# Weaving an expert pair's scatter between the w1/w3 products of the next pair

## What is computed

```python
def _routed_experts(h, expert_id, gate, w1, w3, w2):    # 32 experts, D_EXPERT = 512, 2 experts a token
    ...
    def expert_block(args):
        tok, e, g = args
        xb = h[tok]
        y = (jax.nn.silu(xb @ w1[e]) * (xb @ w3[e])) @ w2[e]
        return (y * g[:, None]).astype(h.dtype)
    ...
    return jnp.zeros_like(h).at[buf_tok].add(y.reshape(P, D))
```

## Time and profile before

| | |
|---|---|
| median of three timed runs | 3413.08 us |
| profiled execution, span | 3411.1 us |
| TensorE busy (products) | 3186.5 us, 93% |
| VectorE, ScalarE, GpSimd busy | 1083.0, 945.4, 884.8 us |
| chain that ended last | TensorE 79%, issue 8%, VectorE 7%, GpSimd 4% |
| expert loop, first w1/w3 load to the last add | about 2735 to 3310 us |

### The profile page before, as it was taken

How to read it: one execution, slowest core, us unless ns; L and a number is a source line. 1 busy time by engine, 2 the same in 40 slices (tenths; PEclk the granted TensorE clock), 3 DMA queues, 4 the chain that set the end, 5 groups by cost and what they waited for, 6 DMA issues and landing times.

```text
span 3411.1 us, 44591 instructions
## 1 busy us (share of the span) xinstructions
PE 3186.5 (93%) x18030; PEld 2437.0 (71%) x18030; DVE 1083.0 (32%) x1746; ACT 945.4 (28%) x1583; POOL 884.8 (26%) x499
## 2 busy tenths in 40 slices
PE   6799999999899999999999999999796899999998
PEld 4687887888788888777888777888573655545543
DVE  2406645112311111141654123212268222222324
ACT  3124444212321122233444233222323111111121
POOL 3331000333322322443100444444564200000000
PEclk9899999999999999998999999999798799999998
DMA  6322221111111111212311222232220478888840
GB/s 208 109 83 92 93 87 57 62 68 62 50 62 51 67 67 52 71 51 82 97 63 56 93 86 86 83 109 83 71 92 13 179 304 363 363 332 363 342 197 25
DMA packets 65557, 415.61 MB, mean 122 GB/s; under 512 B 7648, under 2 KB 9072, under 8 KB 21520
## 3 DMA queue, kind: packets, MB, share of 16 engines
q1 hardware_dynamic: 57600, 393.77, 30.3%
q0 software_dynamic: 5232, 15.64, 2.0%
q10 hardware_dynamic: 2592, 4.34, 0.3%
HBM read 411.61 MB, written 9.96 MB: 124 GB/s over the span
## 4 chain that ended last, share of the span: by engine, by line
PE 79%; issue 8%; DVE 7%; POOL 4%; ACT 2%; ACTq 0%; DMA 0%; POOLq 0%; DVEq 0%
PE ps L500 42%; PE ps L848 7%; PE ps L633 5%; PE ps L648 4%; PE ps L823 4%; PE ps L871 3%; PE ps L671 3%; POOL half_slots L1337 3%; DVE second_block L1798 2%; PE ps L655 2%; PE ps L916 2%; PE ps L888 2%; PE ps L528 2%; DVE X L1971 1%; PE ps L517 1%
## 5 line engine op out<-in xcount | busy, mean ns | idle before, releaser
L500 PE MATMUL ps<-h_parts,half_slots 128*128 128x512 f32 (+1 forms) x6240 | 1230.4, 359 | 68.9 <-POOL half_slots L1337 37.8
L500 PEld LDWEIGHTS ps<-h_parts,half_slots 128*128 128x128 f32 x6240 | 1037.8, 190 | 263.6 <-issue 62.0
L1337 POOL TENSOR_TENSOR half_slots<-ring,half_slots 128x1024 fp32r<-128x1024 f32 (+3 forms) x292 | 630.5, 2160 | 1352.2 <-ACT half_slots L983 1351.9
L983 ACT ACTIVATE half_slots<-ring 128x1024 fp32r<-128x1024 f32 (+3 forms) x292 | 280.3, 961 | 1362.6 <-PE ps L500 1351.7
L500 PE MATMUL ps<-hidden_parts,half_slots 128*128 128x512 f32 (+1 forms) x1584 | 305.1, 355 | 0.0
L500 PEld LDWEIGHTS ps<-hidden_parts,half_slots 128*128 128x128 f32 x1584 | 261.0, 188 | 43.6
L500 PE MATMUL ps<-y_parts,half_slots 128*128 128x512 f32 (+1 forms) x1152 | 230.4, 361 | 10.2 <-DVE y_parts L1652 9.7
L500 PEld LDWEIGHTS ps<-y_parts,half_slots 128*128 128x128 f32 x1152 | 193.9, 192 | 44.7 <-issue 12.0
L848 PE MATMUL ps<-second_block,scratch 128*64 128x512 f32 x1024 | 223.3, 593 | 1.1 <-DVE scratch L1942 0.6
L633 PE MATMUL ps<-half_slots,q_parts 64*128 64x512 f32 (+1 forms) x576 | 183.3, 366 | 6.4 <-DVE na_k_lower L1598 6.2
L1325 POOL COPY second_block<-second_block 128x512 f32<-128x512 f32 x4 | 2.5, 628 | 700.4 <-ACT second_block L952 700.4
(11 more groups left out here) (262 smaller groups left out, 3257.3 us busy)
## 6 DMA issues: line engine op xcount, KB each, us to landing
second_block<-experts SPq DMA_DIRECT2D x192, 1024.0 KB, 7.9
ring<-stream SPq DMA_DIRECT2D x146, 1024.0 KB, 4.8
ring<-stream SPq DMA_DIRECT2D x16, 768.0 KB, 4.1
ring<-stream SPq DMA_DIRECT2D x16, 640.0 KB, 3.8
ring<-stream SPq DMA_DIRECT2D x16, 512.0 KB, 3.4
bias_rows<-rpb POOLq DMA_DIRECT2D x2, 3840.0 KB, 32.6
first_block<-bias_rows POOLq DMA_DIRECT2D x32, 224.0 KB, 4.2
second_block<-w_gate SPq DMA_DIRECT2D x4, 1024.0 KB, 8.0
```

What stands on the lines that cost most here:

```text
L500: last = nc.tensor.matmul(ps[s % 2][:, a:b], part(x, s)[:, k, :], parts[y][:, tile + k, a:b], start=start and k == 0 and n == 0, stop=stop ...
L983: act.activation(part(0, s), raw_half(s), ACT.Copy).then_inc(hi_done, 1)
L1337: nc.gpsimd.tensor_tensor(part(1, s), raw_half(s), part(0, s).bitcast(fp32), ALU.subtract)\
```

## The change

The scatter of pair p is taken out of turn p and put into turn p + 1, on TensorE and on VectorE. On TensorE two tiles of it follow each of the four groups of w1/w3 products: tiles 0 and 1 behind the first, 6 and 7 behind the last. Turn 0 stands ahead of the loop, with nothing to weave; the loop runs `rest` = total - 1 turns; the scatter of the last pair stands behind it, and waits for both copies of the gathered tokens before tile 0. On VectorE a turn begins with the eight adds of the pair before, then come the picks (now of the same turn), GH, the lower part, the copy of gathered tokens, and the selection. `rest` is written into a second element of `total_i` by one more small operation, and TensorE and VectorE read it. ScalarE, GpSimd and SP keep their code.

```diff
--- before.py
+++ after.py
@@ -167,7 +167,7 @@
         es.enter_context(nc.sbuf_tensor("common_memory", [P, 42496], fp32))
         gate = sb("gate", [P, 4, NE])
         pos = sb("pos", [P, 4, NE])
-        total_i = nc.sbuf_tensor("total_i", [P, 1], mybir.dt.int32)
+        total_i = nc.sbuf_tensor("total_i", [P, 2], mybir.dt.int32)
         total_i = es.enter_context(total_i)
         lam8 = sb("lam8", [P, 8, 4])
         vec = sb("vec", [P, NV])
@@ -815,7 +815,8 @@
             pe.wait_ge(htk_a, 4)
             pe.wait_ge(htk_v, 4)
             pe.wait_ge(r_ok, 1)
-            total = pe.value_load(total_i[0:1, 0:1], min_val=PAIRS, max_val=PAIRS * (NL // CAP))
+            rest = pe.value_load(total_i[0:1, 1:2], min_val=PAIRS - 1, max_val=PAIRS * (NL // CAP) - 1)
+            total = rest + 1
 
             def gather(half):
                 for k in range(4 * half, 4 * half + 4):
@@ -833,7 +834,21 @@
             gather(0)
             gather(1)
             turn_selection()
-            with pe.Fori(0, total) as i:
+
+            def scatter(p, tiles):
+
+                for m in tiles:
+                    if m == 0:
+                        pe.wait_ge(m_pick, p + 1)
+                        pe.wait_ge(m_ysv, p + 1)
+                    if m >= 2:
+                        pe.wait_ge(m_add, 8 * p + m)
+                    for x in range(2):
+                        last = nc.tensor.matmul(ps[0][:, 512 * (m % 2):512 * (m % 2) + 512],
+                                                YP[x][:, m // 4, (m % 4) * P:(m % 4 + 1) * P], PICK, start=x == 0, stop=x == 1)
+                    last.then_inc(m_sc, 1)
+
+            def expert_pair(i, before=None):
                 pe.wait_ge(m_xga, i + 1)
                 pe.wait_ge(m_xgv, i + 1)
 
@@ -849,6 +864,8 @@
                                                         XG[:, 4 * kk + k, x * CAP:(x + 1) * CAP], w,
                                                         start=kk == 0 and k == 0, stop=kk == 1 and k == 3)
                         last.then_inc(m_steps, 2)
+                        if before is not None:
+                            scatter(before, (2 * (2 * w13 + kk), 2 * (2 * w13 + kk) + 1))
 
                 pe.wait_ge(m_sel, i + 2)
                 pe.wait_ge(m_add, 8 * i + 1)
@@ -875,19 +892,14 @@
                 gather(1)
 
                 pe.wait_ge(m_w, i + 1)
-                pe.wait_ge(m_pick, i + 1)
                 turn_selection()
 
-                pe.wait_ge(m_ysv, i + 1)
-                for m in range(KD):
-                    if m < 2:
-                        pe.wait_ge((m_xga, m_xgv)[m], i + 2)
-                    if m >= 2:
-                        pe.wait_ge(m_add, 8 * i + m)
-                    for x in range(2):
-                        last = nc.tensor.matmul(ps[0][:, 512 * (m % 2):512 * (m % 2) + 512],
-                                                YP[x][:, m // 4, (m % 4) * P:(m % 4 + 1) * P], PICK, start=x == 0, stop=x == 1)
-                    last.then_inc(m_sc, 1)
+            expert_pair(0)
+            with pe.Fori(0, rest) as i:
+                expert_pair(i + 1, i)
+            pe.wait_ge(m_xga, rest + 2)
+            pe.wait_ge(m_xgv, rest + 2)
+            scatter(rest, range(KD))
 
 
             pe.wait_ge(p_in, 32)
@@ -1915,11 +1927,13 @@
             link(nc.vector.tensor_tensor(passes, passes, gmax[:, 0:1].to_broadcast([P, 8]), ALU.is_lt))
             link(nc.vector.tensor_reduce(gmax[:, 1:2], passes, AX.X, ALU.add))
             link(nc.vector.tensor_scalar(gmax[:, 2:3], gmax[:, 1:2], float(PAIRS), None, ALU.mult))
-            nc.vector.tensor_copy(total_i[:, :], gmax[:, 2:3]).then_inc(r_ok, 1)
+            link(nc.vector.tensor_scalar(gmax[:, 3:4], gmax[:, 2:3], -1.0, None, ALU.add))
+            nc.vector.tensor_copy(total_i[:, :], gmax[:, 2:4]).then_inc(r_ok, 1)
 
 
             dve.wait_ge(r_ok, 1)
-            total = dve.value_load(total_i[0:1, 0:1], min_val=PAIRS, max_val=PAIRS * (NL // CAP))
+            rest = dve.value_load(total_i[0:1, 1:2], min_val=PAIRS - 1, max_val=PAIRS * (NL // CAP) - 1)
+            total = rest + 1
             iota = cst[:, CST["iota"]:CST["iota"] + CAP]
             sel4 = SEL.rearrange("p (c x n) -> p c x n", c=4, x=2)
             selg4 = SELG.rearrange("p (c x n) -> p c x n", c=4, x=2)
@@ -1953,10 +1967,16 @@
                 nc.vector.tensor_tensor(selg4, sel4, wts[:, :, :, None].to_broadcast(shape4), ALU.mult).then_inc(m_sel, 1)
                 nc.vector.tensor_scalar(two, two, -float(CAP), None, ALU.add).then_inc(m_dec, 1)
 
-            gathered(1)
-            picks(1)
-            select_next(1)
-            with dve.Fori(0, total) as i:
+            def add_to_x(p):
+                for m in range(KD):
+                    dve.wait_ge(m_sc, 8 * p + (m + 1))
+                    nc.vector.tensor_tensor(X[:, m, 0:NL], ps[0][:, 512 * (m % 2):512 * (m % 2) + 512], X[:, m, 0:NL],
+                                            ALU.add).then_inc(m_add, 1)
+
+            def expert_pair(i, before=None):
+                if before is not None:
+                    add_to_x(before)
+                picks(i + 1)
                 dve.wait_ge(m_act, i + 1)
                 dve.wait_ge(m_steps, 12 * i + 8)
                 nc.vector.tensor_tensor(GH, ps[1][:, 512:1024], SGM, ALU.mult).then_inc(m_g, 1)
@@ -1966,13 +1986,14 @@
                                                scalar=wslot[:, 0:1], in1=YP[0].bitcast(fp32), op0=ALU.mult,
                                                op1=ALU.subtract).then_inc(m_ysv, 1)
                 gathered(i + 2)
-                for m in range(KD):
-                    dve.wait_ge(m_sc, 8 * i + (m + 1))
-                    nc.vector.tensor_tensor(X[:, m, 0:NL], ps[0][:, 512 * (m % 2):512 * (m % 2) + 512], X[:, m, 0:NL],
-                                            ALU.add).then_inc(m_add, 1)
-                picks(i + 2)
                 select_next(i + 2)
 
+            gathered(1)
+            select_next(1)
+            expert_pair(0)
+            with dve.Fori(0, rest) as i:
+                expert_pair(i + 1, i)
+            add_to_x(rest)
 
             dve.wait_ge(m_add, 8 * total + 1)
             plain_norm(7, "g_ple")
```

## The result

The changed kernel took 3428.65 us (median of 5 runs, 3427.98 to 3430.26), the kernel before beside it 3413.88 (3411.9 to 3415.94): a ratio of 1.0043, 95% interval 1.003 to 1.0055. That is 14.8 us slower; forecast were 3427 and 13.9.

The account below looks back on a forecast made before the run. TensorE, in its order, was taken to set the 35.84 us turn. Terms of 21.03 against 20.24 us gave +0.79 a turn, +11.9 over 15 turns, +2.0 once: +13.9 on the 3413.08 median, 3427 us; range 3414 to 3440.

Parts of the forecast that it names:

- the top: Start of a turn: first w1/w3 product waits for VectorE's gathered-token copy, 1.05 us after the turning's first load.
- four groups of w1/w3: The w1/w3 run cut in four groups of 3.60 us: 14.41 us a turn, the cutting costing 0.50.
- three middle scatters: Four scatter products behind each of the first three w1/w3 groups, 1.15 us each with array-shape switches: 3.45 a turn.
- tiles 6 and 7 and the wait for their adds: Fourth scatter, from tile 6's load to gather(0)'s: 2.12 us for 0.93 us of products.
- the loop entry: Entering the loop of turns: 0.27 us counted once, rounded to +0.3 in the once-per-run sum.
- Rival 1: Array-shape switches between scatter and w1/w3 cost nothing: -0.39 us a turn, 3409 us, no measurable change; chance 0.12 with neighbours.
- The wait at gather(0): gather(0) needs tile 6's bank and waits for all eight adds; some 1.2 us a turn stay on the path.
- Rival 3: The wait at gather(0) costs 0.6 us, not 1.2: 0.19 a turn stays, 3418 us; chance 0.09.
- Rival 2: TensorE's instruction stream falls behind at computed waits: 1.35 us more a turn, 3447 us; chance 0.12, in part or whole.
- Work beside other work: Picks, gated hidden values, selection, silu and weight transfers lie beside other work, at no cost.
- Once per run: Last scatter's first add later by 1.5 us, new small operation +0.2, loop entry +0.3: +2.0 once.
- ring: Scatter tiles wait for adds to free two PSUM banks: 2.2 us of the 5.89 us scatter, which a weave would hide.

Follow-up runs that it names:

- e1: The changed kernel with the waits for the two weight slots put ahead of the waits for the gathered-token copies at a turn's top: 3424.69 us, ratio 1.0029.
- e5: The changed kernel with the weave one group earlier: tiles 0 and 1 ahead of the first w1/w3 group, 6 and 7 behind the third: 3403.37 us, ratio 0.9969.
- e3: The kernel before plus one useless full-width product behind each of the first three groups of w1/w3: 3442.78 us, ratio 1.0084.
- e4: The kernel before plus one useless half-width product behind each of the first three groups of w1/w3: 3424.99 us, ratio 1.0034.
- e7: The changed kernel with a finer weave, one scatter tile behind each of eight half groups of w1/w3: 3448.87 us, ratio 1.0096.
- e2: The changed kernel with scatter tiles in the two ps[2] banks, the wait for adds moved from gather(0) to before w2: 3412.44 us, ratio 0.9994.
- e6: The kernel before, without weave, its scatter using four PSUM banks in place of two: 3385.53 us, ratio 0.9915.

## Why the prediction was right, point by point

| from the turning's first load to gather(0)'s | forecast | measured |
|---|---|---|
| the top, to the first w1/w3 load | 1.05 | 1.33 |
| four groups of w1/w3 | 14.41 | 14.36 |
| three middle scatters | 3.45 | 3.38 |
| tiles 6 and 7 and the wait for their adds | 2.12 | 2.10 |
| sum, against 20.24 before | 21.03 | 21.17 |

- **The top** was the term that was mis-sized, by 0.28 us a turn, 4 us in all. I argued from L871, where three waits stand in a row and cost 0.05. That row was a bad neighbour, but not for the number of its waits: in the built stream nothing is computed between them and the product, while at the top the slots' wait value is computed behind the token waits. The value of turn 0 of before, 0.32, was the right one; it has the same instructions at the top. I had put it down to the loop entry and kept it as the upper end. e1 takes 0.21 of it back (0.35 to 0.14 in the chain); the rest, some 0.07 above the 0.05 that was priced, stays open. The loop entry itself cost nothing: turn 1, the first in the loop, has a top of 1.33 (2766.21 to 2767.54), as the turn shown.
- **Groups and middle scatters** were right to 0.02 us each. A middle scatter is 1.13, in the range of 1.10 to 1.19. The last tile of before took 0.73 to the next half-width load, a lone tile inside the loop 0.66 (e5, tile 1). The 0.07 between them goes with the turn-around and the waits at the top, which no run separates. One reading of the prediction was off in its words alone: in the earlier trace rows four products start between 2661.07 and 2661.77, three steps of 0.23. Rival 1 (switches cost nothing) is refuted by the 1.13 itself, by e3 against e4 and by e7.
- **The wait at gather(0)** was right as a mechanism and in size: 2.10, with 15 waits on VectorE's adds in the profile, and e2 gives 1.1 us a turn back by taking it away. Rival 3 falls with it.
- **Rival 2** (PE's stream falls behind at each computed wait) did not show at the woven tiles: they start without a gap of their own (1.12 to 1.13 in all three middle scatters). Something like it happened at one place only, the top.
- **Work beside other work**: picks, gated hidden values, selection, silu and transfers cost nothing, as said; the time between L876's products and w2 is unchanged, and no transfer ends a wait of TensorE in the turns.
- **Once per run**: +1.16 measured at the last scatter (first load of the turning to first load after the loop: 7.12 before, 8.28 after), forecast +1.5. The rows:

```profile
3318.60 0.69 DVE L1956 COPY scratch<-ps 128x512 f32<-128x512 f32 x1 [1.33 <-PE ps L824]
...
3320.01 0.69 DVE L1967 TENSOR_TENSOR scratch<-scratch,gate 128x512 f32<-128x512 f32 x1
...
3320.69 1.28 DVE L1973 TENSOR_TENSOR X<-ps,X 128x512 f32<-128x512 f32 x2
...
3326.57 0.30 PEld L911 LDWEIGHTS ps<-scratch 128*128 128x128 f32 x2 [1.22 <-DVE X L1973]
```

The selection stands before the first add, as foretold. It takes 1.40 us (3319.29 to 3320.69), but I had counted its 1.5 on top of 0.21 us in which VectorE stood idle before that add anyway, and which it now fills. The +0.3 for the loop entry did not come either.

So the 0.28 that was missed at the top was in part made up for by the other terms of the turn, 0.14 too high together, and by what comes once, forecast at 2.0 and measured at 1.16 in the loop. That 3427 came so close to 3428.65 is in part luck. In all, the weave took 2.2 us of ring out of a turn and put in 1.17 at gather(0), 0.9 at the top, and three switches there and back at 0.36.

## What to carry to other kernels

Here the stall of a ring of buffers was better removed with more buffers than by weaving other work in, since banks were free at that time: four banks gave 29 us, the best place for the weave 11, the weave as made lost 15. Before moving a step into a gap, look at what stands right behind the new place and right behind the old one: the wait at the top had been hidden by the step that was moved, the wait at gather(0) by the products that it was moved past, and moving the same weave by one group turned the loss into a gain. Weaving products of two array shapes has a price per switch, so weave seldom and in large pieces.

## What the runs showed of the hardware that I had not expected

The price of a switch of array shape hardly depends on what is around it: 0.36 us there and back from e3 against e4 with a product of 128 columns, 0.35 from e7 and about 0.34 from e5 against e6 with the scatter's own, and the first load after a half-width group comes at the same 0.81 us of idle load time in all of them, before a scatter, a lone product or a gather.

A wait value that is computed in the instruction stream can cost time at a wait that stands ahead of it. Where the computation stood behind the wait that ended last, the product came 0.35 us after the releaser; with it ahead of that wait 0.14 (e1). Where nothing was computed the load came after 0.07 (turn 0 of the changed kernel, four waits) and 0.05 (w2, three waits). So in these runs it paid to write the waits with values yet to be computed first, and the wait that ends last behind them.
